# Six edits to the order of work ahead of the expert loop of a decoder layer with 32 experts

## What is computed

```python
logits = (xt @ w_router) + b_router              # 1024 tokens, 32 experts
top_vals, top_idx = lax.top_k(logits, 4)
gates = softmax(top_vals)
# each expert takes its tokens, in blocks:
h = xblk @ w1[e] + b1[e]                         # 1024 -> 2048
y = clamped_swiglu(h) @ w2[e] + b2[e]            # 1024 -> 1024
out[token] += gate * y                           # on top of the residual h
```

## Time and profile before

| | us |
|---|---|
| median of 3 runs | 2222.09 (2217.77 to 2222.6) |
| span of the profiled execution | 2218.5 |
| PE busy | 2134.6 (96%) |
| DVE busy | 1476.1 (67%) |
| ACT busy | 1175.5 (53%) |
| POOL busy | 211.6 (10%) |
| mean DMA rate | 215 GB/s |

### The profile page before, as it was taken

The page is one execution under the profiler, slowest core; times in us unless marked ns, Lnnn a source line. Parts: engine busy times, 40 slices in busy tenths (PEclk is TensorE's granted clock), DMA queues, the critical chain, the costliest instruction groups (busy, mean ns, idle before and its releaser), DMA issues.

```text
span 2218.5 us, 35301 instructions
## 1 busy us (share of the span) xinstructions
PE 2134.6 (96%) x11434; PEld 1690.3 (76%) x11435; DVE 1476.1 (67%) x2300; ACT 1175.5 (53%) x1619; POOL 211.6 (10%) x204
## 2 busy tenths in 40 slices
PE   6999998997899999999999999999999999999997
PEld 4443787444688977977888888887779978898895
DVE  3241584446876678778767676769886667567666
ACT  3241452114665477567555555567774555556545
POOL 2000200002110011011101001010100110101001
PEclk9999997998999999999999999999999999999999
DMA  7000402002996589879968686768997667658556
GB/s 262 1 0 19 162 1 76 29 29 71 343 371 187 195 272 376 285 237 330 348 209 302 210 295 210 280 221 314 367 349 255 212 217 286 192 183 323 184 189 224
DMA packets 203285, 477.88 MB, mean 215 GB/s; under 512 B 14775, under 2 KB 20983, under 8 KB 203184
## 3 DMA queue, kind: packets, MB, share of 16 engines
q1 hardware_dynamic: 185758, 438.21, 54.4%
q0 software_dynamic: 17424, 39.17, 7.3%
q10 hardware_dynamic: 66, 0.02, 0.0%
HBM read 468.99 MB, written 32.11 MB: 226 GB/s over the span
## 4 chain that ended last, share of the span: by engine, by line
PE 80%; DVE 6%; issue 5%; DMA 4%; ACT 3%; DVEq 1%; ACTq 1%; POOLq 0%; POOL 0%; SPq 0%
PE ps L1199 18%; PE ps L1201 18%; PE ps L1200 18%; PE ps L950 7%; PE ps L1104 5%; DMA out<-y,idx_cur 3%; PE ps L1312 3%; DVE w_lo L1735 2%; PE ps L1193 1%; PE ps L1055 1%; PE ps L1023 1%; PE ps L1242 1%; DVE xT L1735 1%; PE ps L1262 1%; ACT w_hi L817 1%
## 5 line engine op out<-in xcount | busy, mean ns | idle before, releaser
L817 ACT ACTIVATE w_hi<-ring 128x1024 fp32r<-128x1024 f32 x730 | 781.6, 1122 | 419.3 <-PE ps L1201 372.4
L1735 DVE TENSOR_TENSOR w_lo<-ring,w_hi 128x1024 fp32r<-128x1024 f32 x732 | 862.3, 1220 | 191.1 <-ACT w_hi L817 191.0
L1199 PE MATMUL ps<-xT,w_hi 128*128 128x256 f32 x1248 | 354.2, 284 | 0.0
L1201 PE MATMUL ps<-xT,w_lo 128*128 128x256 f32 x1248 | 353.1, 283 | 0.0
L1200 PE MATMUL ps<-xT,w_hi 128*128 128x256 f32 x1248 | 353.1, 283 | 0.0
L1199 PE MATMUL ps<-w_hi,xT 128*128 128x512 f32 x816 | 323.0, 396 | 12.6 <-issue 7.1
L1200 PE MATMUL ps<-w_lo,xT 128*128 128x512 f32 x816 | 319.2, 391 | 0.0
L1201 PE MATMUL ps<-w_hi,xT 128*128 128x512 f32 x816 | 319.0, 391 | 0.0
L1199 PE MATMUL ps<-w_hi,actT 128*128 128x512 f32 x644 | 262.8, 408 | 0.0
L1201 PE MATMUL ps<-w_hi,actT 128*128 128x512 f32 x644 | 251.6, 391 | 0.0
L1200 PE MATMUL ps<-w_lo,actT 128*128 128x512 f32 x644 | 251.1, 390 | 0.0
(11 more groups left out here) (284 smaller groups left out, 2364.7 us busy)
## 6 DMA issues: line engine op xcount, KB each, us to landing
ring<-in_w SPq DMA_DIRECT2D x390, 1024.0 KB, 7.9
xh<-in_x SPq DMA_DIRECT2D x4, 2048.0 KB, 15.8
work<-in_w_out SPq DMA_DIRECT2D x1, 4096.0 KB, 12.7
token_rows<-uT POOLq DMA_DIRECT2D x8, 512.0 KB, 2.9
out<-xh SPq DMA_DIRECT2D x8, 512.0 KB, 9.0
work<-in_w_in SPq DMA_DIRECT2D x2, 1536.0 KB, 18.4
uT<-in_w_mem_kv SPq DMA_DIRECT2D x1, 2048.0 KB, 13.8
ring<-in_w_in SPq DMA_DIRECT2D x1, 1536.0 KB, 18.4
```

The costliest lines, as they stand in the source:

```text
L817: act_e.activation(hi, raw, ACT.Copy).then_inc(hi_ready, counted(h, whole))
L1199: pe.matmul(acc, hi, whi, start=first, stop=False, skip_group_check=shared)
L1201: return pe.matmul(acc, lo, whi, start=False, stop=last, skip_group_check=shared)
L1735: return dve.tensor_tensor(lo, x, hi.bitcast(F32), ALU.subtract)
```

## The change

Six edits, none inside the loop's body:

1. ScalarE: the two roundings of the gates come ahead of all four `first_hi`, not between the third and the fourth.
2. VectorE: the low words of the gates come ahead of the first one-hot, not behind it.
3. GpSimd: the four low words of weights come ahead of the wait for the pass table and of the memsets of `limit`, not behind them.
4. GpSimd makes the low words of b1, behind those memsets; it waits for its own earlier work and for ScalarE's rounding of b1 first.
5. VectorE no longer makes the low words of b1. Its waits for them and for the memsets at the loop's entry stay.
6. TensorE: the wait for the pass table and the read of the number of passes come ahead of the waits for the initial rows.

```diff
@@ gpsimd
             po.wait_ge(idx_ready, 1)
             gather_x()
-            po.wait_ge(ttab_ready, 1)
-            po.memset(limit[:, 0, :], LIMIT).then_inc(zeroed, 1)
-            po.memset(limit[:, 1, :], LIMIT + 1.0).then_inc(zeroed, 1)
             for s in range(LEAD_POOL):
                 po.wait_ge(hi_ready, s + 1)
                 po.tensor_tensor(halves_of(w_lo[s][:, :, :]), pairs_apart(part(s)), halves_of(w_hi[s][:, :, :].bitcast(F32)),
                                  ALU.subtract).then_inc(raw_done[s // 2], 1)
+            po.wait_ge(ttab_ready, 1)
+            po.memset(limit[:, 0, :], LIMIT).then_inc(zeroed, 1)
+            po.memset(limit[:, 1, :], LIMIT + 1.0).then_inc(zeroed, 1)
+            po.wait_ge(raw_done[1], 2)
+            po.wait_ge(zeroed, 4)
+            po.wait_ge(b1_hi, 2)
+            b1_words = b1w[E:2 * E, :].rearrange("p (j two c) -> p j two c", j=4, two=2)
+            po.tensor_tensor(b1_words, b1_raw[E:2 * E, :].rearrange("p (j c two) -> p j two c", j=4, two=2),
+                             b1_words.bitcast(F32), ALU.subtract).then_inc(b1_lo, 1)
+            po.wait_ge(b1_lo, 1)
             po.wait_ge(init_out, 16 * NT)
@@ scalar
-            first_hi(0)
-            first_hi(1)
-            first_hi(2)
             act_e.wait_ge(gates_ready, 1)
             for k in (0, 2):
                 act_e.activation(gates3_r[:, :, k, :], gates[:, :, :], ACT.Copy).then_inc(g_hi, 1)
-            first_hi(3)
+            for s in range(4):
+                first_hi(s)
@@ tensor
+            pe.wait_ge(ttab_ready, 1)
+            total = pe.value_load(ttab[0:1, TALL:TALL + 1], min_val=1, max_val=NPASS)
             pe.wait_ge(init_a, NA)
             pe.wait_ge(init_d, 2 * NT - NA)
-            pe.wait_ge(ttab_ready, 1)
-            total = pe.value_load(ttab[0:1, TALL:TALL + 1], min_val=1, max_val=NPASS)
@@ vector
-            onehot_of(iota_s[:, 0:PASS], slice(0, 1))
             dve.wait_ge(g_hi, 2)
             dve.tensor_tensor(gates3_r[:, :, 1, :], gates[:, :, :], gates3[:, :, 0, :], ALU.subtract).then_inc(g_lo, 1)
+            onehot_of(iota_s[:, 0:PASS], slice(0, 1))
             make_idx(1, 2)
@@ vector
-            dve.wait_ge(b1_hi, 2)
-            b1_words = b1w[E:2 * E, :].rearrange("p (j two c) -> p j two c", j=4, two=2)
-            minus_hi(b1_words, b1_raw[E:2 * E, :].rearrange("p (j c two) -> p j two c", j=4, two=2),
-                     b1_words).then_inc(b1_lo, 1)
```

## The result

| | before | after |
|---|---|---|
| median, us | 2220.6 (2217.77 to 2222.6, 4 runs) | 2229.36 (2226.83 to 2232.89, 4 runs) |
| span of the profiled execution, us | 2218.5 | 2225.6 |

The ratio is 1.0042 with a 95% interval of 1.0026 to 1.0058: slower by 5.8 to 12.9 us. (The median of before moved from 2222.09 to 2220.6, because one more run stood beside the changed kernel.)

The account below looks back on a forecast made before the run. TensorE, four fifths of the span, was taken as the bound, its loop start set by VectorE's pass table. +8.6 (step 4) - 1.3 (step 1) + 0 (steps 2, 3) = +7.3 us on 2222.1: 2229.4, range 2220.5 to 2232.0.

Parts of the forecast that it names:

- step 4: GpSimd's four low words ahead of the pass table block four VectorE operations there: 8.6 us later, bounds 0 and 9.6.
- the bound of 9.6: Upper bound for GpSimd's low words beside the pass table: one VectorE operation waits through all four, 9.6 us.
- step 1: TensorE reads the pass count beside its wait for the initial rows: gain 1.3 us, bounds 1.1 and 1.4.
- Rival D: As C, and the loop's first products find the higher clock level: -2.9 us, 2219.2; chance 0.04.
- Step 2: Gates' rounding on ScalarE and low words on VectorE come earlier: index ready within 0.2 us of now, sum 0.
- Step 3: Biases' low words move from VectorE to GpSimd, 4.8 us there: cost 0 while GpSimd finishes before VectorE enters the loop.
- A: The forecast: two-input and one-source pass-table operations are both blocked, +7.3 us, own range 2227.5 to 2231.5; chance 0.53.
- B: One-column pass-table operations L1706 and L1712 run free, later ones are held: +5.0 us, 2227.1; chance 0.15.
- C: Not slower: at most one pass-table operation blocked, price 0 to 1.9 us, net -1.3 to +0.6, 2220.8 to 2222.7; chance 0.25.

Follow-up runs that it names:

- run with gaps: Changed kernel plus a GpSimd wait for its own completion after each of the four low words; ratio to before 1.0038 (1.0025 to 1.005).
- memsets: Changed kernel with GpSimd's four low-word subtractions replaced by memsets of zero over the same tiles; 2221.72 us in a single run (before: 2221.99).
- two ahead: Changed kernel with only two of GpSimd's four low words ahead of the wait for the pass table; ratio to before 1.0017 (1.0008 to 1.0026).

## Why the prediction was right, and where it was only nearly right

**Sign, kind of mechanism and place: right.** The forecast was 2229.4, measured 2229.36. The loss was put on step 4, GpSimd's subtractions beside the pass table, and the runs with this edit undone and with it alone agree. That four hundredths of a microsecond separate the two is luck: the forecast was 7.3 us on top of 2222.1, and what was measured is 8.8 on top of a median of before that is 1.5 lower; the profiled span rose by 7.1, the stretch from the gates to pass 2 by 9.0, and the passes behind it were 1.6 shorter in the trace of after, which is scatter.

**Step 4, how the wait falls: wrong as a picture, mis-sized as a term.** The prediction said that the waiting one comes next, and gave four waits of up to 2.39 us for L1706, L1709, L1710 and L1712 (before's numbers), 8.6 us in all. Instead all four kept 0.16 to 0.24, and one operation ahead of them, L1702, took the whole run. The term is 10.18 - 0.19 = 9.99 us. It is above the bound of 9.6 too: the hold was there 0.67 us before GpSimd's recorded start, and so it hit L1702, which the prediction had counted as done. The prediction's own sign of being wrong, L1709 and L1710 at 0.24 and 0.19, came half true: they kept these times, but behind GpSimd's run (555.36 and 555.64 against its end at 554.27), not beside it. The reading that failed was that of the earlier trace rows: L1574 was let in between L503 and L505, but there GpSimd waits for its own result between the two. The run with gaps shows that this makes the difference, and there the waiting is 8.45 us, close to the 8.6 of the prediction. The other row, L1628 in the earlier trace rows, sat through two GpSimd operations, and the prediction used it for the bound only; it was the better row. The 9.0 us at pass 2 are made up of 9.99 for this wait, less 0.27 for the earlier index and 1.35 for step 1, plus 0.63 lost again at the lower clock.

**Step 1: right.** 1.3 forecast; the issue gap fell from 5.82 to 4.47. It reaches the product with `sel` only in part: from the first product to that one it takes 5.18 us in the changed kernel against 4.55 before, so 0.63 of the 1.35 is lost again, because twelve products instead of nine ran 0.43 us apart, at the lower clock level (granted clock 0.50 from 571 to 574 and 0.51 from 574 to 576.9). Rival D had hoped for the opposite. It isn't bound to the shorter gap either: the runs with gaps, memsets and two ahead, with gaps of 4.08, 3.68 and 4.51 us, needed 4.45, 4.31 and 4.44.

**Step 2: within 0.1 of its bound, and not quite nothing.** The index is ready 4.32 us from the gates' last operation, 4.59 before (540.48 + 0.16 - 536.32, 541.14 + 0.16 - 536.71): 0.27 earlier, where up to 0.2 was allowed. No wait hides it; it is the reason why L1192 came 9.72 and not 9.99 later from the gates.

**Step 3: right for the changed kernel, for a reason the prediction gave only as a condition.** GpSimd took 4.66 (4.8 forecast), VectorE's splits ran undisturbed (2.35) and `sel` ended 1.3 us ahead of need. With GpSimd's low words behind the table the same edit costs 1.15 us.

**The rivals.** A has the right time and the right kind of hold, but not the four waits. (Its lower edge was mis-added: two of the four waits half as long take off some 2.2 us, which gives 2227.2 and not 2227.5.) B is refuted: one-column operations with two inputs are held (1.77 and 2.02 us). (In its sum the table is 6.4 us late, 556.1 - 549.70, and not 6.3.) The row on which it rested, L1540, is not explained by its size; in the run with gaps L1716 got through in the same way, right behind another VectorE operation. C's condition, at most one operation of the table blocked, came true by its words; what failed is its price, 0 to 1.9 us for one operation, where the one cost 9.99. That price had counted on a wait behind one GpSimd operation only, and its reason, that short two-input operations are not held, is refuted. Something like C's time is what a GpSimd that only writes gives: 79.42 at pass 2 against 79.33; the block of 2.84 us there is mostly paid for by an issue gap of 3.68 us in place of 5.82 and by the earlier index. D did not come: the clock was not up at the first products.

## What to carry to other kernels

When work is moved on GpSimd, look at what VectorE does in the new place, not at whether GpSimd was idle: an operation of 0.19 us on the critical path can stand behind everything that GpSimd has queued back to back. Its price is the length of GpSimd's whole run. If the overlap can't be avoided, a wait between the pieces lets VectorE take turns; here that took 1.5 us of 10 off in the trace, and nothing that the end time shows. Operations that read one operand from PSUM are the ones to put beside GpSimd: the tokens' low words took VectorE 1.23 us beside GpSimd's subtractions in before and 1.22 us beside an idle GpSimd in the changed kernel. Before's order made use of that, and its 9.55 us of GpSimd cost it only 0.9 us of VectorE's biases (3.20 us, against 2.28 in the run with the low words ahead alone).

## What the runs showed of the hardware that was not expected

- VectorE can be held before GpSimd's operation starts by the record. In the changed kernel L1707 starts at 544.13, while the gather's record still runs to 544.77, and is held; GpSimd's first subtraction is recorded from 544.80. With the subtractions behind the table, the same product starts at 544.28 beside the same gather (543.92 to 544.93) and takes 0.19. So it is the queued subtraction and not the gather that holds it, 0.67 us ahead of its record in three traces (544.13 and 544.80, 546.85 and 547.52, 546.73 and 547.40). The lead is not always there: with a wait between GpSimd's operations, L1716 started at 552.38, just ahead of the fourth subtraction's record at 552.39, and took 0.19. GpSimd's records are rough, so whether the hold comes early or the record late is not shown.
- Between GpSimd operations that stand back to back, where GpSimd waits only for semaphores reached long before, a waiting VectorE operation was not let in: 10.18 us for four, 5.50 for two, 3.08 for four memsets. With a wait of GpSimd on its own result between them it was, each time.
- A one-source operation of one column was not held, neither beside memsets nor beside a subtraction (0.15 us each). One of 32 columns was, beside both (3.08 and 2.27 us).
- The stage of 530 us ahead of the change ends up to 4.96 us apart from execution to execution (534.18 to 539.14). In the trace with the earliest gates TensorE's granted clock was 0.93 from 300 to 400 us, in all the others 0.86. What decides that was not looked into.
- The way from the first product to the one with `sel`, where TensorE waits at most 0.2 us for anything else, took 4.31 to 5.46 us, by how many of its products ran at the lower clock level. It did not follow from the length of the issue gap ahead: 5.82 us gave 4.55, 4.47 gave 5.18, 3.68 gave 4.31. This stays open.
